# Zero-filled 128-partition tiles for the gating bias and the gate vectors, and gated branches with tokens on the partitions

## The reference

```python
# first block, gated MLP: positions of a chunk of 128 are mixed per group g, with a bias per position
sp = jnp.einsum('gts,bcsgd->bctgd', w_s, gv) + b_s.T[:, :, None]
y_gmlp = gu * sp.reshape(Bq, S, D_GMLP)
...
# first block, mLSTM: a row per head, the negated running maximum m_t, enters the exponents
Wqk = jnp.exp(Dm - m_t[..., None]) * jnp.einsum('bhctd,bhcsd->bhcts', q, k)
...
# second block, each layer: three branches, each with its own sigmoid gate of 1024 columns
gates = jax.nn.sigmoid(gate_logits).reshape(B, L, N_BRANCHES, D_MODEL)
merged = (gates[:, :, 0] * (y_hy @ w_br_hyena[i])
          + gates[:, :, 1] * (y_gla @ w_br_gla[i])
          + gates[:, :, 2] * (y_pool @ w_br_pool[i]))
x = x + _rms_norm(merged @ w_out[i], norm_mix_post[i])
```

## Time and profile before

| | |
|---|---|
| three executions | 1675.16, 1679.55, 1678.46 us |
| profiled execution | 1678.48 us |
| its span | 1676.7 us |
| granted TensorE clock, mean | 0.987 |
| TensorE busy | 1620.0 us (97%) |
| VectorE busy | 937.6 us (56%) |
| ScalarE busy | 731.7 us (44%) |
| GpSimd busy | 93.2 us (6%) |
| moved by DMA | 399.41 MB, 238 GB/s over the span |

### The profile page before, as it was taken

The page is one execution under the profiler, slowest core; times in us unless marked ns, Lnnn a source line. Parts: engine busy times, 40 slices in busy tenths (PEclk is TensorE's granted clock), DMA queues, the critical chain, the costliest instruction groups (busy, mean ns, idle before and its releaser), DMA issues.

```text
span 1676.7 us, 24633 instructions
## 1 busy us (share of the span) xinstructions
PE 1620.0 (97%) x10153; PEld 1246.7 (74%) x10153; DVE 937.6 (56%) x1608; ACT 731.7 (44%) x1423; POOL 93.2 (6%) x81
## 2 busy tenths in 40 slices
PE   7999997999999999979999999999989999999998
PEld 6987884443434433328999998999879999989997
DVE  5966655223232323118676567766666755677665
ACT  6754542101111011118664347655666643475554
POOL 1010001000000000003200000000132000000000
PEclk9999998999999999999999999999999999999999
DMA  8433486999999999993444454455534444545450
GB/s 351 175 126 108 167 329 239 380 343 423 424 424 400 424 424 424 425 364 142 149 150 170 152 185 181 176 191 187 185 129 148 162 167 150 189 174 191 177 193 33
DMA packets 57279, 399.41 MB, mean 238 GB/s; under 512 B 6597, under 2 KB 7014, under 8 KB 9804
## 3 DMA queue, kind: packets, MB, share of 16 engines
q1 hardware_dynamic: 57164, 397.80, 61.5%
HBM read 396.72 MB, written 1.05 MB: 237 GB/s over the span
## 4 chain that ended last, share of the span: by engine, by line
PE 91%; DVE 3%; DMA 3%; ACT 2%; issue 1%; POOL 0%; SPq 0%; DVEq 0%
PE P L171 89%; DMA RING<-in_ws_dram 3%; PE P L174 2%; DVE X L189 0%; DVE RINGL L183 0%; ACT WH L177 0%; ACT HT L177 0%; DVE X L183 0%; DVE GS L183 0%; DVE SM L189 0%; ACT JNK L177 0%; DVE YB L183 0%; ACT L180 0%; DVE RT L189 0%; POOL RINGL L183 0%
## 5 line engine op out<-in xcount | busy, mean ns | idle before, releaser
L183 DVE TENSOR_TENSOR RINGL<-RING,WH 128x1024 fp32r<-128x1024 f32 x338 | 417.8, 1261 | 143.9 <-ACT WH L177 143.1
L171 PE MATMUL P<-HA,WH 128*128 128x256 f32 x1592 | 454.3, 285 | 0.0
L171 PE MATMUL P<-LA,WH 128*128 128x256 f32 x1592 | 448.5, 282 | 0.0
L171 PE MATMUL P<-HA,RINGL 128*128 128x256 f32 x1592 | 448.4, 282 | 0.0
L177 ACT ACTIVATE WH<-RING 128x1024 fp32r<-128x1024 f32 x351 | 357.9, 1054 | 5.0 <-DMA RING<-in_ws_dram 2.7
L171 PEld LDWEIGHTS P<-HA,WH 128*128 128x128 f32 x1592 | 300.2, 189 | 6.3 <-issue 3.5
L171 PEld LDWEIGHTS P<-HA,RINGL 128*128 128x128 f32 x1592 | 301.0, 189 | 2.6 <-issue 0.5
L171 PEld LDWEIGHTS P<-LA,WH 128*128 128x128 f32 x1592 | 301.3, 189 | 0.0
L171 PE MATMUL P<-RING,XT 128*64 128x512 f32 x632 | 145.7, 598 | 2.2 <-DMA RING<-in_ws_dram 2.2
L171 PEld LDWEIGHTS P<-RING,XT 128*64 128x64 f32 x632 | 43.0, 136 | 87.5 <-issue 78.7
L189 DVE SCALAR_TENSOR_TENSOR YSL<-P,SM,YSH 128x512 fp32r<-128x512 f32 x32 | 22.5, 746 | 108.8 <-ACT YSH L177 108.8
(11 more groups left out here) (405 smaller groups left out, 2660.4 us busy)
## 6 DMA issues: line engine op xcount, KB each, us to landing
RING<-in_ws_dram SPq DMA_DIRECT2D x288, 1024.0 KB, 4.9
ew<-in_ws_dram SPq DMA_DIRECT2D x47, 1024.0 KB, 18.5
ez<-in_ws_dram SPq DMA_DIRECT2D x16, 1024.0 KB, 18.8
ek<-in_ws_dram SPq DMA_DIRECT2D x6, 1024.0 KB, 9.9
ef<-in_ws_dram SPq DMA_DIRECT2D x4, 1024.0 KB, 10.9
eha<-in_ws_dram SPq DMA_DIRECT2D x2, 1024.0 KB, 4.8
ela<-in_ws_dram SPq DMA_DIRECT2D x2, 1024.0 KB, 6.9
TAB<-in_dft_dram SPq DMA_DIRECT2D x2, 1024.0 KB, 6.2
```

The lines of the kernel that those rows point to most:

```text
L171: return self.engine.matmul(*a, **k) if self.engine else self
L183: return self.engine.tensor_tensor(*a) if self.engine else self
```

## The change

**Tiles.** `BS` and `NC` become tiles of 128 partitions (the same bytes on each). GpSimd fills both with zeros at the start; the bias is loaded into partition 0 of `BS` behind that fill, and VectorE writes partitions 0 to 3 of `NC` behind its fill. The products that read them now name all 128 partitions: ones (128 x 128) x `BS`, and one-hot (rows 4 to 127 zero) x `NC`. The sums are the same.

**Branches.** Gates and branches are made by `stream_rows`, for a half h of 512 columns at a time: four gate chunks, then two branch chunks. The weights are packed in that order. `GSB` and `MG` now hold tokens on the partitions, so `MG` is transposed by TensorE before `wo` (`tensor_merged_turn`: 16 transposes a layer, in two turns of 8), and ScalarE and VectorE split the transposed value from PSUM. The number of chunks, their bytes and the work on high and low parts stay.

```diff
-        self.NC = z("NC", [4, 2, 256])
+        self.NC = z("NC", [128, 2, 256])
-        self.BS = z("BS", [1, 4, 128])
+        self.BS = z("BS", [128, 4, 128])
...
-    e.dma_start(m.BS[:, :, :], A["b_s"]).then_inc(*s.b_s_in.up(0))
+    e.wait_ge(*s.cleared_p["BS"])
+    e.dma_start(m.BS[0:1, :, :], A["b_s"]).then_inc(*s.b_s_in.up(0))
...
     e.memset(m.ONEROW[:, :], 1.0).then_inc(*s.cleared_p.up("ONEROW"))
+    e.memset(m.BS[:, :, :], 0.0).then_inc(*s.cleared_p.up("BS"))
+    e.memset(m.NC[:, :, :], 0.0).then_inc(*s.cleared_p.up("NC"))
...
-        p = e.matmul(m.P[5][:, d * 256:(d + 1) * 256], m.con("onehot", h * 128, h * 128 + 128, p=4), m.NC[:, d, :],
+        p = e.matmul(m.P[5][:, d * 256:(d + 1) * 256], m.con("onehot", h * 128, h * 128 + 128), m.NC[:, d, :],
...
-            p = e.matmul(out, m.con("ones", p=1), m.BS[:, g, :], start=False, stop=True)
+            p = e.matmul(out, m.con("ones"), m.BS[:, g, :], start=False, stop=True)
...
+    e.wait_ge(*s.cleared_p["NC"])
-    e.tensor_scalar(m.NC[:, :, :], m.FG[:, :, :], -1.0, None, ALU.mult).then_inc(*s.vec.up("nc"))
+    e.tensor_scalar(m.NC[0:4, :, :], m.FG[:, :, :], -1.0, None, ALU.mult).then_inc(*s.vec.up("nc"))
...
-    gate = lambda which, i: stream_t(e, m, s, chunk(which, 3 * (i // 2) + i % 2), a, (s.evac, ("sigmoid", l, which, i)))
-    branch = lambda which, x, p: stream_t(e, m, s, chunk(which, 3 * p + 2), x,
-                                          (s.merged if which == "pb" else s.drain, (l, which, p)), kt=4, parts=2)
+    def gate(which, h, j):
+        stream_rows(e, m, s, gate_chunks(l, which, h), j, a, lambda t: (s.evac, ("sigmoid", l, which, h, t)))
+    def branch(which, x, h):
+        done = s.merged if which == "pb" else s.drain
+        for j in range(2):
+            stream_rows(e, m, s, branch_chunks(l, which, h), j, x, lambda t: (done, (l, which, h, t)))
...
+    for j in range(4):
+        gate("hb", 0, j)
+    branch("hb", hy, 0)
+    gate("hb", 1, 0)
+    gate("hb", 1, 1)
+    tensor_merged_turn(e, m, s, l, 0)
+    gate("hb", 1, 2)
+    gate("hb", 1, 3)
+    branch("hb", hy, 1)
...
     for j in range(4):
         stream_rows(e, m, s, range(chunk("wo"), chunk("wo") + 4), j, y, lambda t: (s.drain, ("post", l, 0, t, 0)))
+        if j == 0:
+            tensor_merged_turn(e, m, s, l, 1)
...
+def tensor_merged_turn(e, m, s, l, h):
+    for i in (2 * h, 2 * h + 1):
+        b = 4 + i
+        for k in (2 * i, 2 * i + 1):
+            for t in range(2):
+                e.wait_ge(*s.merged[l, "hb", h, t])
+                for sig, event in m.free[b]:
+                    e.wait_ge(*sig[event])
+                p = e.transpose(m.P[b][:, (k % 2) * 256 + t * 128:(k % 2) * 256 + t * 128 + 128],
+                                m.MG[:, t, k * 128:(k + 1) * 128], m.con("ident"))
+        p.then_inc(*s.turn.up("merged", l, i))
+        m.free[b] = [(s.act_lo, ("merged", l, i))]
...
+def scalar_merged(e, m, s, l, h):
+    for i in (2 * h, 2 * h + 1):
+        e.wait_ge(*s.turn["merged", l, i])
+        e.wait_ge(*s.drain["spectrum", l, 1, 0])
+        e.activation(m.HB[:, 2 * i:2 * i + 2, :], m.P[4 + i][:, :].rearrange("p (k t) -> p k t", k=2),
+                     ACT.Copy).then_inc(*s.act_hi.up("merged", l, i))
...
+def vector_branch(e, m, s, l, which, h):
+    chunks = branch_chunks(l, which, h)
+    lo_until(e, m, s, chunks[1] + 5)
+    for t in range(2):
+        g, sum_ = m.GSB[:, t, :], m.MG[:, t, h * 512:(h + 1) * 512]
+        e.wait_ge(*s.stream[chunks[1] if t else ("t0", chunks[1])])
+        e.wait_ge(*s.evac["sigmoid", l, which, h, t])
+        product = m.P[m.bank[chunks[0], t]][:, :]
+        if which == "pb":
+            e.tensor_tensor(sum_, product, g, ALU.mult).then_inc(*s.merged.up(l, which, h, t))
+        else:
+            e.tensor_tensor(g, product, g, ALU.mult).then_inc(*s.drain.up(l, which, h, t))
+            e.wait_ge(*s.drain[l, which, h, t])
+            e.tensor_tensor(sum_, sum_, g, ALU.add).then_inc(*s.merged.up(l, which, h, t))
```

More of the change, by code:

```diff
@@ L817, in stream_rows @@
 def stream_rows(e, m, s, chunks, j, a, freed, pairs=(0, 1, 2, 3)):
+    end = len(chunks) - 1
     if j == 0:
@@ L830, in stream_rows @@
             ta = slice(t * 128, (t + 1) * 128)
-            first, last = j == 0 and i == 0, j == 3 and i == 1
+            first, last = j == 0 and i == 0, j == end and i == 1
             sig, event = a.hi_mark(k, t)
@@ L847, in stream_rows @@
     p.then_inc(*s.stream.up(c))
-    if j == 3:
+    if j == end:
         m.held.discard(b)
@@ L2913, in tensor_layer @@
+    gate("pb", 0, 0)
+    gate("pb", 0, 1)
     tensor_gla_turn(e, m, s, l)
+    gate("pb", 0, 2)
+    gate("pb", 0, 3)
     branch("pb", pool, 0)
[L2915 to L2918, removed]
+    for j in range(4):
+        gate("pb", 1, j)
+    branch("pb", pool, 1)
     tensor_spectrum(e, m, s, l, 0)
-    gate("gb", 0)
-    gate("gb", 1)
+    gate("gb", 0, 0)
+    gate("gb", 0, 1)
     tensor_spectrum(e, m, s, l, 1)
+    gate("gb", 0, 2)
@@ L2923, in tensor_layer @@
+    gate("gb", 0, 3)
     branch("gb", gla, 0)
-    gate("gb", 2)
-    gate("gb", 3)
-    branch("gb", gla, 1)
[L2927 to L2940, removed]
+    gate("gb", 1, 0)
@@ L3306, in scalar_layer @@
                          scale=m.par(f"gla_norm{l}")).then_inc(*s.act_hi.up("gla", l, h))
[L3307 to L3310, removed]
+    scalar_gate(e, m, s, l, "pb", 0)
+    scalar_gate(e, m, s, l, "pb", 1)
+    scalar_gate(e, m, s, l, "gb", 0)
+    hi_until(e, m, s, chunk("gb", 7) + 5)
     for i in range(2):
@@ L3315, in scalar_layer @@
             e.activation(m.HH[:, c, :], m.X0[:, c, :], ACT.Copy).then_inc(*s.act_hi.up("hy", l, c))
[L3316 to L3326, removed]
+    scalar_gate(e, m, s, l, "gb", 1)
+    scalar_gate(e, m, s, l, "hb", 0)
+    hi_until(e, m, s, chunk("hb", 7) + 5)
+    scalar_merged(e, m, s, l, 0)
+    scalar_gate(e, m, s, l, "hb", 1)
+    hi_until(e, m, s, chunk("wo") + 5)
+    scalar_merged(e, m, s, l, 1)
     e.preload_act_table_set("natural_log_exp_and_others")
@@ L3448, in scalar_hyena, with scalar_gate @@
                  scale=m.par(f"hcw{l}", 12 + i)).then_inc(*s.evac.up("hy", l, i))
[L3451 to L3461, removed]
+def scalar_gate(e, m, s, l, which, h):
+    chunks = gate_chunks(l, which, h)
+    hi_until(e, m, s, chunks[3] + 5)
+    before = {"pb": None, "gb": "pb", "hb": "gb"}[which]
+    for t in range(2):
+        e.wait_ge(*s.stream[chunks[3] if t else ("t0", chunks[3])])
+        if h:
+            e.wait_ge(*s.merged[l, which, 0, t])
+        elif before:
+            e.wait_ge(*s.merged[l, before, 1, t])
+        e.activation(m.GSB[:, t, :], m.P[m.bank[chunks[0], t]][:, :],
+                     ACT.Sigmoid).then_inc(*s.evac.up("sigmoid", l, which, h, t))
+def scalar_merged(e, m, s, l, h):
[4 more added lines that the diff above has]
+                     ACT.Copy).then_inc(*s.act_hi.up("merged", l, i))
 def scalar_post(e, m, s, l, w, t, n, bank):
```

69 lines of the change are left out of this document (34 added, 35 removed).

## The result

The changed kernel takes **1666.16 us** (median of 4 executions, 1664.48 to 1666.65). The kernel before, on the same chip, took 1677.93 us (median of 4). The ratio is 0.993, 95% interval 0.9913 to 0.9947: 11.8 us less, where 3.2 us were predicted.

The account below looks back on a forecast made before the run. TensorE, busy in 97% of the span, was taken to bound the kernel through the order and distance of its matmuls. The terms -3.1 - 3.8 + 3.7 = -3.2 us gave 1675.3 us, range 1670.5 to 1680.5.

Parts of the forecast that it names:

- Work on the array does not change: Spatial product: filling `BS` and `NC` leaves 16 records at 3.32 us at full clock, 0.21 us each.
- I cost them at nothing: Kernel start: the two zero fills, SyncE's one wait and VectorE's wait for `NC` were put at no cost.
- VectorE does not allow all of it: First block's mixer: VectorE can start only 1.95 us earlier and `V` x `MN` waits, so 3.1 of 4.5 us is gained.
- new wait of 1.4 us: First block's mixer: the rest of the 4.5 us was to become a new wait for VectorE.
- Part 1: Zeros in `BS` and `NC`, spatial product and next chunk: gain 3.1 us, ends 0 and 4.5 us.
- The clock's part: From 121.74 to 131.98 us: 128 rows, 127 of them zeros, keep 2.4 GHz, worth 2.29 + 2.20 = 4.5 us.
- rival 1: Spatial product: rows of zeros don't count as work, the clock falls as before, gain 0: 1678.4 us; chance 0.18.
- Part 2: Branches in two layers: chunks of 12 matmuls of 512 columns gain 3.8 us, added transposes lose 3.7 us: 0.1 us.
- rival 2: Tiles and branches both give their upper end, 4.5 and 1.8 us, together 6.3: 1672.2 us; chance 0.24.
- The cover: Start of `wo`: its first chunk of 2.80 us hides the 2.4 us until `MG` is whole; slack 0.4 us.
- two groups of three matmuls: End of the branches: the first half of the tokens ends that far ahead of the branch's end, 0.7 us.

Follow-up runs that it names:

- e1_tiles: The kernel before with the zero-filled 128-row tiles for both the bias (`BS`) and the head rows (`NC`), branches as before: 1668.53 us, ratio 0.9946.

## Why the prediction was wrong, point by point

- **The step that failed**: "Work on the array does not change", a term put at nothing. The 3.32 us of the 16 records at full clock were read as the array's own work, and half of them was the price of 8 changes of row count. With 128 rows in each the work is 1.71 us. The evidence stood in the earlier trace rows: eight records `V` x `MN`, just as wide, take 0.81 us, 0.10 each. Two numbers for one kind of work in one group ask for an explanation. This is 3.2 us over the two halves.
- "I cost them at nothing" stood for the fills; the gate rows got no term at all. Four heads gain 0.3 to 0.4 us each, 1.5 us together, of which a longer wait at 110 us takes 0.4 back: 1.2 us net by the kernel with that tile alone.
- **"VectorE does not allow all of it"** was wrong. `V` x `MN` doesn't wait for the `MN` that ends at that point but for that of the head before. No new wait of 1.4 us formed; what grew is the wait for `MN` near 110 us, from 0.5 to 0.9 us. The clock gave its whole 4.4 us (2.29 + 2.12).
- Part 1 by rows: 3.2 + 4.4 + 1.5 for the head rows + 0.1 for the product behind the first half, less 0.45 us that the first half lost and 0.4 us at 110 us: 8.35 us, beside 8.34 measured and 3.1 predicted. The first half took 2.16 us and not 1.71, since TensorE had to wait before 118.17 us for `GV`, on which GpSimd worked until 118.12 us (an operation of 2.13 us here, of 1.28 us in the kernel before and in `e1_tiles`, where the first half takes 1.78 us):

```profile
115.99 2.13 POOL L183 TENSOR_TENSOR GV<-GV,LNB 128x512 f32<-128x512 f32 x1
```
- **The clock's part was right**: 128 rows, most of them zeros, keep it up, and rival 1, *Zeros don't count*, falls. The Trainium skill, "TensorE: Matmul & The Clock Gate", section "What's actually happening", says that the gate follows how busy the engine has been; read plainly, an engine that is already busy can't be made busier by zeros, which would have given 0. The runs disagree with that reading: 1.00 with zeros in 128 rows, 0.50 with zeros in 1 row, busy in every microsecond of both stretches.
- **Part 2 was right in form and off by 1.9 us.** The 36 chunks of layer 0 take 101.29 us, taking out what stands between them; 100.7 was forecast. But before they took 103.85 us where I took 102.6 from three chunks in a row in gb (8.55 us): the chunks next to a transform or a turn cost more, so that the 12 of gb take 35.22 us and not 34.2. So the gain is 2.6 us a layer for 1.9. A turn takes 0.79 us (below) where I took 0.92. Net 1.0 us a layer instead of 0.05, near the 1.8 us for both layers that rival 2 gave. In the run with the branches alone the trace shows about 1.0 us in each of the two stages; its gain of 3.4 us in the median has shifts outside them in it (0.9 us in the experts, 0.9 us between the layers).

```profile
972.21 1.04 PE L174 MATMUL P<-CONS,MG 128*128 128x128 f32 x8
973.00 0.48 PE L171 MATMUL P<-WH,HA 128*128 128x512 f32 x1
```

- **The cover was right.** (The prediction counts "two groups of three matmuls" for the 0.7 us between the two halves of the tokens; 0.7 us is one group, and the trace shows one.) VectorE now, where `hb` ends:

```profile
983.78 0.69 DVE L183 TENSOR_TENSOR GSB<-P,GSB 128x512 f32<-128x512 f32 x1 [0.96 <-PE P L171]
984.51 0.69 DVE L183 TENSOR_TENSOR MG<-MG,GSB 128x512 f32<-128x512 f32 x1
985.12 0.68 DVE L183 TENSOR_TENSOR GSB<-P,GSB 128x512 f32<-128x512 f32 x1
985.83 0.69 DVE L183 TENSOR_TENSOR MG<-MG,GSB 128x512 f32<-128x512 f32 x1
```

`wo` begins at 984.28 and `MG` is whole at 986.52, 2.24 us later (forecast 2.4); the second turn starts at 987.08 and waits for nothing. No wait of TensorE stands between 870 and 1000 us.
- The range was too narrow because part 1 had only one unknown in it, the clock, with ends at 0 and 4.5 us. The direct effect of the edit on its own products had no upper end at all.

## What to carry to other kernels

A small fp32 product of few rows between 128-row products is paid at both of its edges, 0.2 us each, more than its own work (two records of 0.11 us). Next to products that fill 64 columns of the array nothing was paid. Filling it up to 128 rows with zeros cost nothing on the array here and removed both; where that isn't possible, put the small ones side by side. Not where two of them stand on different rows and run together: there, filling loses. And before a number in a row is taken for an engine's own work, find the same work elsewhere in the trace and ask why it differs.

## What was not expected of the hardware

- The change of row count costs about 0.2 us (0.19 to 0.24 by the place), the same for 1, 32 and 64 rows against 128. The Trainium skill, "TensorE: Matmul & The Clock Gate", section "LDWEIGHTS (loading the stationary operand)", says that a load of 32 rows takes as long as one of 128. That speaks of a load by itself, and within a run of one count it agrees (1-row records as fast as 128-row ones); at a change it misses 0.2 us.
- The clock can be halved for 27 and 37 us under an engine that is busy without a gap, if most of its records use 1 row (or 1 and 128 in turn); one execution each.
- Near that edge the fall is a matter of the single execution: one kernel's ten times stand in two groups some 5 us apart or more, with a gap between 1672.72 and 1676.38 us.
